# A second mixer in one block: scans among the projection's chunks, local attention by pairs of heads

## The reference

```python
proj = h @ w_in[l]                                  # 512 x 1280
u, q, k, v = jnp.split(proj, [D_SSM, D_SSM + D_ATTN, D_SSM + D_ATTN + KV_DIM], axis=-1)
...
bu_re = jnp.einsum("blgh,gph->blgp", ug, bb_re)     # 32 groups x 64 complex states
_, _, s_re, s_im = lax.associative_scan(combine, (a_re_t, a_im_t, bu_re, bu_im), axis=1)
y = (einsum(s_re, c_re) - einsum(s_im, c_im) + d_skip * ug)
...
q, k = _rms(q, q_norm_w[l]), _rms(k, k_norm_w[l])   # 8 query heads, 2 key heads of 64
logits = jnp.where(mask, q @ k.T * 64 ** -0.5 + bias, -1e30)   # 128 queries x 256 keys
m = jnp.maximum(jnp.max(logits, axis=-1, keepdims=True), sink)
p = jnp.exp(logits - m)
probs = p / (jnp.sum(p, axis=-1, keepdims=True) + jnp.exp(sink - m))
```

## Time and profile before

| | us |
|---|---|
| median of three runs (1416.92 to 1420.22) | 1418.18 |
| the profiled execution, its own time | 1418.51 |
| span of that execution (first to last instruction) | 1416.6 |
| PE busy / VectorE / ScalarE / GpSimd | 1289.3 / 804.6 / 514.8 / 137.1 |

### The profile page before, as it was taken

The page is one execution under the profiler, slowest core; times in us unless marked ns, Lnnn a source line. Parts: engine busy times, 40 slices in busy tenths (PEclk is TensorE's granted clock), DMA queues, the critical chain, the costliest instruction groups (busy, mean ns, idle before and its releaser), DMA issues. The chain is left out here.

```text
span 1416.6 us, 15641 instructions
## 1 busy us (share of the span) xinstructions
PE 1289.3 (91%) x6274; PEld 990.7 (70%) x6274; DVE 804.6 (57%) x1299; ACT 514.8 (36%) x817; POOL 137.1 (10%) x129
## 2 busy tenths in 40 slices
PE   6999997879999899999998975678979999999999
PEld 5786564538788678888876762346758887888877
DVE  5557664134655844656547956754875553355632
ACT  5345456544322211222224532346343441244321
POOL 0000000013200700000014700001510000000000
PEclk9999998979999989999998986589999999999999
DMA  8311112012344345444442510010212212322232
GB/s 347 106 53 38 60 61 90 1 60 80 131 168 147 106 151 205 157 156 138 149 149 67 125 31 0 1 61 30 90 46 103 90 62 102 119 89 90 71 101 82
DMA packets 24328, 138.44 MB, mean 98 GB/s; under 512 B 2973, under 2 KB 4189, under 8 KB 14912
## 3 DMA queue, kind: packets, MB, share of 16 engines
q1 hardware_dynamic: 23488, 135.81, 27.7%
q0 software_dynamic: 768, 1.63, 1.0%
HBM read 133.75 MB, written 3.67 MB: 97 GB/s over the span
## 5 line engine op out<-in xcount | busy, mean ns | idle before, releaser
L121 ACT ACTIVATE w_hi_part<-w_raw 128x2048 fp32r<-128x2048 f32 (+1 forms) x101 | 175.3, 1735 | 308.4 <-PE bank L135 296.0
L133 PE MATMUL bank<-xhi_ffn,w_hi_part 128*128 128x512 f32 x704 | 280.2, 398 | 6.6 <-DVE xlo_ffn L235 6.6
L135 PE MATMUL bank<-xhi_ffn,w_lo_part 128*128 128x512 f32 x704 | 278.5, 396 | 0.0
L134 PE MATMUL bank<-xlo_ffn,w_hi_part 128*128 128x512 f32 x704 | 278.3, 395 | 0.0
L127 DVE TENSOR_TENSOR w_lo_part<-w_raw,w_hi_part 128x2048 fp32r<-128x2048 f32 (+1 forms) x101 | 212.4, 2103 | 106.5 <-ACT w_hi_part L121 103.2
L133 PEld LDWEIGHTS bank<-xhi_ffn,w_hi_part 128*128 128x128 f32 x704 | 132.7, 188 | 38.7 <-issue 7.6
L135 PEld LDWEIGHTS bank<-xhi_ffn,w_lo_part 128*128 128x128 f32 x704 | 132.6, 188 | 31.9
L134 PEld LDWEIGHTS bank<-xlo_ffn,w_hi_part 128*128 128x128 f32 x704 | 132.8, 189 | 31.2 <-issue 0.2
L356 DVE SCALAR_TENSOR_TENSOR squares<-bank,param,squares 128x511 f32<-128x511 f32 x88 | 63.9, 747 | 91.3 <-ACT squares L339 89.8
L133 PE MATMUL bank<-hhi_half,w_hi_part 128*128 128x512 f32 x240 | 96.8, 404 | 6.5 <-DVE hlo_half L331 6.5
L133 PE MATMUL bank<-hhi,w_hi_part 128*128 128x512 f32 x240 | 95.9, 400 | 1.3 <-DVE hlo L364 1.3
(11 more groups left out here) (338 smaller groups left out, 2092.8 us busy)
## 6 DMA issues: line engine op xcount, KB each, us to landing
mod_w<-in_w_mod SPq DMA_DIRECT2D x32, 768.0 KB, 4.4
w_raw<-in_w_gu SPq DMA_DIRECT2D x22, 1024.0 KB, 4.8
w_raw<-in_w_down SPq DMA_DIRECT2D x32, 704.0 KB, 4.1
w_raw<-in_w_up SPq DMA_DIRECT2D x22, 1024.0 KB, 4.8
w_raw<-in_w_in_f SPq DMA_DIRECT2D x9, 1024.0 KB, 5.2
w_raw<-in_w_out SPq DMA_DIRECT2D x8, 1024.0 KB, 4.7
w_raw<-in_w_in SPq DMA_DIRECT2D x5, 1024.0 KB, 4.8
x<-in_x SPq DMA_DIRECT2D x4, 512.0 KB, 8.6
```

The lines of the kernel that those rows point to most:

```text
L121: act.activation(k.whi[:, slot, 0:width], k.raw[:, slot, 0:width], ACT.Copy).then_inc(k.w_hi, 1)
L133: pe.matmul(out, whi, xhi, start=first, stop=False)
L134: pe.matmul(out, whi, xlo, start=False, stop=False)
L135: return pe.matmul(out, wlo, xhi, start=False, stop=last)
```

## The change

Both blocks become one, without the barrier. What changes in it:

- The key and value chunk of the projection moves from the fifth to the third place (`IN2_AT`).
- The scan's inputs are made by PE behind the second and the third chunk, `spin` follows on VectorE between the chunks' rest parts, and both scans run whole, before attention begins.
- VectorE first waits for the `time` tile and copies the position column into PSUM (`clock`); its angle operations read it there. It does so before it scales the input.
- The DMAs of the bias table move from GpSimd's queue to SP's, and GpSimd no longer waits for the table's rows before the second part of its work.
- Attention is written anew, in 16 steps of one pair of heads each, instead of 32 of one head. The sink is column 257 of the bias, beside a zero score, so the maximum and the sum contain it without operations of their own. The negation, the reciprocal and the copy of the turned tile are one instruction for a pair.
- PE is one pair ahead with its scores. The outputs of the scan are divided into two parts (`lags`, `from_states`) behind different steps.
- Head norms are in two groups, the second one's reciprocal inside attention; weights `GLU`, `OUT2` and `OUT2 + 2` all use the first slot, while the second holds the scan's states.

The diff, cut to its core:

```diff
+        states = [over("states0", [P, 2, 8, NCK], raw_at + 4 * TILE),
+                  powers[:, 0:2, :, :, :].rearrange("p n a t c -> p n (a t) c")]
+        spin_tmp = k.sq[:, :, :].rearrange("p (a s) (t c) -> p a (s t) c", a=2, c=NCK)
...
+        clock = k.bank[6][:, 0:NCK]
+        y_bank = k.bank[6]
+        in_banks = (k.bank[2], k.bank[3], k.bank[4], k.bank[5])
+        score_bank = ((k.bank[4], k.bank[5]), (k.bank[0], k.bank[1]))
...
+
+                def load(n, src):
+                    sp.wait_ge(k.w_lo, n - 1 if raw_of(n) == raw_of(n - 2) and raw_of(n - 1) != raw_of(n) else n)
+                    sp.dma_start(k.raw[:, raw_of(n), :], src).then_inc(k.w_loaded[n % 2], 16)
+
+                load(IN2 + 4, io["w_in2"][IN2_AT[4]])
+                sp.wait_ge(rel_sb, 1)
+                sp.dma_start(io["rel_scratch"], rel_rows[:, :].unsqueeze(1).broadcast_to([8, P, 384])).then_inc(rel_out, 16)
+                sp.wait_ge(rel_out, 16)
+                sp.wait_ge(rel_made, 1)
+                sp.wait_ge(time_set, 1)
+                sp.wait_ge(turned, 4)
+                sp.wait_ge(c_taken, 1)
+                sp.dma_start(bias2[:, :, 0:256], bass.AP(io["rel_scratch"].tensor, io["rel_scratch"].offset + P - 1,
+                                                         [[383, P], [P * 384, 8], [1, 256]])).then_inc(rel_in, 16)
+                load(GLU, io["w_glu"])
+                load(OUT2, io["w_out2"][0])
+                load(OUT2 + 2, io["w_out2"][2])
+                sp.wait_ge(y_made, 2)
+                load_chunk(sp, k, 1, io["w_out2"][1], after_lo=OUT2)
+                sp.wait_ge(c_in, 32)
+                sp.wait_ge(rel_in, 16)
...
+                pool.sem_inc(c_taken, 1)
...
+                turns(0)
+                turns(1)
+                act.wait_ge(k.w_used, IN2 + 1)
+                first_tile(IN2, 0, k.bank[0])
+                next_weights(IN2 + 2)
+                act.wait_ge(rel_made, 1)
+                act.activation(rel_rows[:, :], k.bank[3][0:8, 0:384], ACT.Copy).then_inc(rel_sb, 1)
+                sines(0)
+                for a in range(2):
+                    act.wait_ge(bt_made, a + 1)
+                    act.activation(bt[:, a, :], k.bank[4 + a][:, :], ACT.Copy).then_inc(bt_sb, 1)
+                sines(1)
+                first_tile(IN2 + 1, 2, k.bank[0])
+                turns(2)
+                turns(3)
+                next_weights(IN2 + 3)
+                sines(2)
+                sines(3)
+                first_tile(IN2 + 2, 8, k.bank[0])
+                act.wait_ge(evac2a, 3)
+                square(0)
+                next_weights(IN2 + 4)
...
+                next_weights(GLU)
+                act.wait_ge(h2_sum, 3)
+                act.activation(root_a[0:96, :], k.bank[7][0:96, :], ACT.Sqrt, bias=eps_col[0:96, 0:1],
+                               scale=1.0 / HD).then_inc(h2_root, 1)
+                first_tile(IN2 + 4, 6, k.bank[0])
...
+                next_weights(OUT2)
+                act.wait_ge(h2_sum, 5)
+                act.activation(root_b[0:64, :], k.bank[7][0:64, :], ACT.Sqrt, bias=eps_col[0:64, 0:1],
+                               scale=1.0 / HD).then_inc(h2_root, 1)
...
+                def bias(p):
...
+                        dve.wait_ge(l_scored, u + 1)
+                        dve.tensor_tensor_reduce(prob2[:, s, at:257], score_bank[p % 2][r][:, at:257],
+                                                 bias2[:, h, at:257], 1.0, NEG, ALU.add, ALU.max,
+                                                 k.nmax[:, u:u + 1]).then_inc(l_biased, 1)
+                    dve.wait_ge(l_biased, 2 * p + 2)
+                    dve.tensor_scalar(k.nmax[:, 2 * p:2 * p + 2], k.nmax[:, 2 * p:2 * p + 2], -1.0, None,
+                                      ALU.mult).then_inc(l_maxed, 1)
...
+                dve.wait_ge(c_in, 32)
+                dve.tensor_copy(clock, chunk_time).then_inc(time_set, 1)
...
+                angle(0)
+                angle(1)
+                second_tile(IN2, 1)
+                next_rest(IN2 + 2)
+                cosine(0)
+                cosine(1)
+                angle(2)
+                angle(3)
+                second_tile(IN2 + 1, 3)
+                next_rest(IN2 + 3)
+                cosine(2)
+                cosine(3)
+                dve.wait_ge(k.w_lo, IN2 + 4)
                 spin(0)
+                dve.wait_ge(k.w_used, IN2 + 3)
+                dve.tensor_copy(v2[:, :, :], k.bank[7][:, :].rearrange("p (i n) -> p i n", n=P)).then_inc(evac2v, 1)
+                next_rest(IN2 + 4)
+                spin(1)
...
+                for b in (4, 5):
+                    dve.memset(k.bank[b][:, 256:257], 0.0).then_inc(l_zero, 1)
+                second_tile(IN2 + 3, 5)
+                scan(0)
+                next_rest(GLU)
+                scan(1)
                 dve.wait_ge(h2_root, 1)
-                dve.reciprocal(root10[:, :], root10[:, :]).then_inc(h2_inv, 1)
...
+                dve.reciprocal(root_a[0:96, :], root_a[0:96, :]).then_inc(h2_inv, 1)
+                second_tile(IN2 + 4, 7)
+                scale_head2(0)
...
+                scale_head2(1)
...
+                scale_head2(2)
                 dve.wait_ge(rel_in, 16)
...
+                chain.link(dve.tensor_copy(bias2[:, :, 256], pr("sinks")))
+                for p in range(PAIRS + 1):
+                    if p < PAIRS:
+                        bias(p)
+                    if p >= 1:
+                        normalise(p - 1)
+                    if p == 0:
+                        next_rest(OUT2)
+                        dve.wait_ge(h2_root, 2)
+                        dve.reciprocal(root_b[0:64, :], root_b[0:64, :]).then_inc(h2_inv, 1)
+                    if p == 2:
+                        scale_head2(3)
+                    if p == 3:
+                        scale_head2(4)
+                    if p < 8:
+                        for part in range(3 * (p % 2), 3 * (p % 2) + 3):
+                            spin_back(p // 2, part)
+                    if p in (6, 9, 12, 15):
+                        output((6, 9, 12, 15).index(p))
...
+                pe.wait_ge(k.w_lo, IN2 + 2)
+                pe.wait_ge(evac2a, 1)
+                features(IN2 + 1, 0).then_inc(half_made, 1)
+                pe.wait_ge(evac2v, 1)
+                features(IN2 + 1, 1).then_inc(k.w_used, 1)
+                pe.wait_ge(rel_sb, 1)
+                pe.wait_ge(bt_sb, 2)
                 inputs(0)
...
+                n = IN2 + 2
+                pe.wait_ge(k.w_lo, n + 1)
+                pe.wait_ge(evac2a, 2)
+                features(n, 0).then_inc(half_made, 1)
+                pe.wait_ge(evac2v, 2)
...
+                pe.wait_ge(v_turned, 4)
                 inputs(1)
...
+                pe.wait_ge(k.w_lo, IN2 + 4)
+                pe.wait_ge(evac2a, 3)
+                features(IN2 + 3, 0).then_inc(half_made, 1)
...
+                features(IN2 + 4, 0).then_inc(half_made, 1)
+                pe.wait_ge(evac2v, 4)
+                for m in range(3):
+                    sums2(m, 3)
+                features(IN2 + 4, 1).then_inc(k.w_used, 1)
+                pe.wait_ge(v_turned, 8)
+                wide2(0)
+                wide2(1)
                 lag_weights()
...
+                pe.wait_ge(h2_root, 1)
+                for m in range(3, 5):
+                    sums2(m, 2)
+                wide2(2)
+                pe.wait_ge(h2_done, 2)
+                pe.wait_ge(h2_scaled, 3)
+                pe.wait_ge(l_zero, 4)
+                pe.wait_ge(h2_root, 2)
+                scores(0)
+                for p in range(PAIRS + 1):
+                    if p + 1 < PAIRS:
+                        scores(p + 1)
+                    if p < PAIRS:
+                        turn(p)
+                    if p in (1, 2):
+                        wide2(2 + p)
+                    if p == 3:
+                        pe.wait_ge(h2_scaled, 5)
+                    if p and p % NT == 0:
+                        values(p // NT - 1)
+                    if p in (2, 7, 10, 13):
+                        lags((2, 7, 10, 13).index(p))
+                    if p in (5, 8, 11, 14):
+                        from_states((5, 8, 11, 14).index(p))
```

More of the change, by code:

```diff
@@ L41, with __init__ @@
 class Unit:
-    def __init__(self, branch, i, q, key, width, blocks, table, gate=None, sink=None, nsink=None):
+    def __init__(self, branch, i, q, key, width, blocks, table, gate=None):
         self.branch, self.i, self.q, self.key, self.width, self.blocks = branch, i, q, key, width, blocks
-        self.table, self.gate, self.sink, self.nsink = table, gate, sink, nsink
+        self.table, self.gate = table, gate
 class Branch:
@@ L548, in normalise @@
             dve.wait_ge(exped, u + 1)
-            if unit.sink is not None:
-                chain.link(dve.tensor_tensor(k.rsum[:, u:u + 1], k.rsum[:, u:u + 1], k.esink[:, u:u + 1], ALU.add))
             chain.link(dve.reciprocal(k.rsum[:, u:u + 1], k.rsum[:, u:u + 1]))
```

(25 more changed lines are left out.)

553 lines of the change are left out of this document (271 added, 282 removed).

## The result

The changed kernel took 1435.2 us (median of 4 runs, 1431.95 to 1439.15), the kernel before 1419.2 (now of 4 runs as well). The ratio is 1.0118 (95% interval 1.0095 to 1.0142). Forecast was 1427 with a range of 1405 to 1440: slower, as said, but by 16 us and not by 8. It lies inside that range and 1 us outside the narrower one of 1420 to 1434 that had a chance of 0.50. A second job with the changed kernel gave 1.0111 (1.0075 to 1.0147), so the size is firm.

What follows compares the result with a forecast made beforehand. Bound: PE in the projection, PE and VectorE by turns until first scores, then VectorE and later PE's products in attention. Start +12.8, up to scores -11.7, attention 102.1 against 94.8: +8.4 on 1418.51, forecast 1427 us, range 1405 to 1440.

Steps and rivals of the forecast that it cites:

- the value products: Projection, value half of the key chunk on PE: 10.8 us, as in the kernel before.
- PE's blocks in attention: Attention, between turning and next scores, added in full: values 9.6, lags 14.4, products from states 7.7, spreads 3.0 us.
- The path and the waits: PE's steps in order, with 3.4 us waiting for ScalarE's copy, and waits for VectorE in each attention step.
- Start of the mixer: VectorE's input scaling waits for the position copy, then runs wholly beside GpSimd: slower by 12.8 us on PE's path.
- From there to the first scores: Removed barrier, hidden `inputs` and spins gain 11.7 us; first scores at 870.5 against 869.4, net +1.1.
- rival 3: Table holds SP's queue, so the gate's weights land late and the second scan shifts about 5 us: 1432; chance 0.10.
- Attention: First scores to the end of attention: slower, 102.1 us against 94.8.
- the chain: Attention: scores, bias, scaling and turning run one after the other each step; fourteen steps 53.9 us, less 4.4: 49.5.
- A light step: Attention step without other work on PE: 3.85 us, between 4.35 at the lower clock and 3.3 at the upper.
- Rival 1: PE keeps the upper clock in the attention loop: 85 us in place of 102, 1410 in all; chance 0.21.
- Rival 2: Angles still run slowly beside GpSimd, 9.85 us and not 3.41, twice: +12.9, 1440; chance 0.07.
- Rival 4: Nothing moves: start costs less as GpSimd finishes in 33 us, attention steps cost 3.4: 1418; chance 0.12.

Runs made afterwards that it cites:

- Two experiments with different edits: Changed kernel with the position column's copy moved behind the split: 1.0035, 1423.6 us; changed kernel with GpSimd held until the split is done: 1.0005, 1420.9 us.
- two pairs ahead: Changed kernel with PE's scores two pairs ahead of the turning, not one, and six slots of probabilities, not four: 0.9945, 1410.3 us.
- the experiment with SBUF: Changed kernel with the angles read from the position column in SBUF, not from its PSUM copy: 1443.4 us in one execution.
- the two combined ones: Changed kernel with late copy, GpSimd held, early table, state products behind lags, scores two pairs ahead: 1388.9 us; the same with three places mended: 1382.4 us.

## Why the prediction was right in sign and half in size

The medians lie 8.2 us above the forecast, and the mixer accounts for 7.3 of them: 2.8 before the first scores and 4.5 in attention. The steps that failed are two terms taken from rows of the kernel before: the value products (10.8 us, measured 15.2) and PE's blocks in attention (34.7 us, measured 41.8). The path and the waits were right.

- **Start of the mixer: right.** The wait, the contention and PE's wait for ScalarE came as worked out: first chunk ended at 31.5 us for 31.4, PE waited 2.93 for 3.4. Two experiments with different edits took 13.6 and 14.6 us back.
- **From there to the first scores: a term was mis-sized.** The step "half a chunk and the values 5.7 + 10.8" took the earlier trace rows as they stood. The values took 15.2, because of the stop and the lower clock behind it. All else on the path held: a chunk of 11.3, `inputs` 7.6 and 7.7, and from the fourth chunk's end VectorE's chain 16.3 us for the 17.1 forecast. Result 121.0 for 118.2. In the kernel before the table's transfer was issued at 772.9 and ended at 772.9 + 36.6 = 809.5, just ahead of these products; I had put it at 835 in rival 3 and asked only which transfer it held up, not what else lay beside it. That rival did not come true: the gate's weights landed in 7.7 us and VectorE's rest at 855.32 waited for nothing.
- **Attention: the chain was right, the blocks' clock was not.** A light step was put at 3.85 us at a mixed clock, and 3.2 to 3.6 were measured. The blocks were put at 9.6 + 14.4 + 7.7 + 3.0 = 34.7 us and took 9.6 + 17.3 + 10.8 + 4.1 = 41.8. I took the lags at less than their row's 4.04, for a part at the upper clock (in the kernel before one of four took 2.58), and the products from the states at 1.94, a row that stood right behind the lags. The change parts them. All four lags ran at a granted clock of 0.50 to 0.60, 4.25 to 4.48 us each, and two of the four products from the states at 0.53 and 0.58. Putting the latter back behind the lags gave 3.2 us back; the lags' 2.9 and the spreads' 1.1 were not tested apart. Together +7.1 in blocks and -2.6 in the rest: the loop took 4.5 more than forecast.
- **Rival 1** (the upper clock in the loop) is refuted: 0.70, about what the forecast had. It named the point where this turns, steps under 3.3 us, and two pairs ahead went past it: 0.81, a loop of 79.4 us, 1410.3.
- **Rival 2** is refuted by the groups of 2.3 us, which is even less than the 3.41 that I took; its size was put at 12.9 us, and the experiment with SBUF showed 9.3.
- **Rival 4** (the start costs less as GpSimd finishes early) is refuted: the sixteen operations lay wholly beside GpSimd.

## What to carry to other kernels

A small copy at the head of an engine's queue costs more than its own wait if it moves the work behind it beside an engine that it contends with; look at what will then run side by side. In a software pipeline over two engines, count the steps that the chain goes through per turn: one more pair in flight was worth 27 us here, over half of it through the clock. A block's duration is only good for the place that its row stood in: right behind the lags 64 small products took 1.94 us, all at 2.4 GHz; set apart from them two of four took 3.3 to 3.6, mostly at 1.2.

## What was new of the hardware

- The 1.5 MB table, written in small pieces for 35 us at about 49 GB/s, goes with a stop of 0.85 to 1.26 us on PE, at one fixed place of the program for a given order, and the granted clock falls behind it (0.50 for 7.2 us in the changed kernel, 0.56 to 0.80 for 3 us in the two combined ones). A 16 KB packet of the instruction queue, some 12 us later in the changed kernel than with the transfer moved, starts 2.3 to 2.5 us before each stop ends. The stop is short; in the changed kernel what follows cost four times as much.
- A `scalar_tensor_tensor` of 128x128 took 0.29 us with a PSUM and an SBUF source (2.29 for eight), beside GpSimd or not, 0.38 with two SBUF sources, and 1.1 to 1.2 with these beside GpSimd (8.80 and 9.85 for eight).
- The clock behind the mixer differed between two executions of the same kernel (0.89 and 0.77 over 30 us), which is worth 3 to 4 us at the end: one profile of each kernel is not enough to place the last 0.2%.
